# The second channel block of a causal depthwise convolution: from VectorE to GpSimd

## The reference, cut to what matters

```
def causal_dwconv(x, buf, w, b):
    xp = jnp.concatenate([buf.astype(x.dtype), x], axis=1)
    y = lax.conv_general_dilated(xp, w[:, None, :], window_strides=(1,), padding='VALID', ..., feature_group_count=x.shape[-1])
    return y + b.astype(x.dtype), xp[:, -(w.shape[0] - 1):]
...
glu = b_in[..., :W_B] * jax.nn.sigmoid(b_in[..., W_B:])          # W_B = 256
cb, nbuf_b = causal_dwconv(glu, buf_b, cm_dw_w[l], cm_dw_b[l])   # 31 taps
out_b = jax.nn.silu(layernorm_f32(cb.astype(jnp.float32), cm_ln_g[l], cm_ln_b[l]))
```

## Time and profile before

| what | value |
|---|---|
| median of 3 timed runs | 981.76 us (980.2 to 981.83) |
| span of the profiled execution | 979.8 us |
| outside that span, against the median | 2.0 us |
| TensorE busy | 922.9 us, 94% |
| VectorE busy | 453.6 us, 46% |
| GpSimd busy | 144.7 us, 15% |
| mean granted clock of TensorE | 0.974 |

### The profile page before, as it was taken

The page is one execution under the profiler, slowest core; times in us unless marked ns, Lnnn a source line. Parts: engine busy times, 40 slices in busy tenths (PEclk is TensorE's granted clock), DMA queues, the critical chain, the costliest instruction groups (busy, mean ns, idle before and its releaser), DMA issues.

```text
span 979.8 us, 13718 instructions
## 1 busy us (share of the span) xinstructions
PE 922.9 (94%) x5196; PEld 505.3 (52%) x5196; DVE 453.6 (46%) x1013; ACT 167.6 (17%) x357; POOL 144.7 (15%) x185
## 2 busy tenths in 40 slices
PE   7999779889999999999989997898799999999996
PEld 6744434675545545455476444347555554545552
DVE  3378794443343343434324887826224334343435
ACT  2213121201111111111211221211011111111113
POOL 0101110041112121211010001101311212121200
PEclk9999979899999999999999998899999999999999
DMA  9944622649999999993873055327499999999811
GB/s 301 312 167 188 165 87 60 237 153 372 378 390 359 389 374 373 398 360 142 280 235 129 1 218 128 92 43 306 173 389 391 386 389 374 379 388 358 341 65 49
DMA packets 100879, 252.76 MB, mean 258 GB/s; under 512 B 31682, under 2 KB 65494, under 8 KB 84438
## 3 DMA queue, kind: packets, MB, share of 16 engines
q1 hardware_dynamic: 73502, 239.45, 64.0%
q10 hardware_dynamic: 22728, 8.02, 3.6%
q0 software_dynamic: 4608, 4.73, 1.6%
HBM read 258.13 MB, written 6.52 MB: 270 GB/s over the span
## 4 chain that ended last, share of the span: by engine, by line
PE 76%; issue 13%; DVE 5%; ACTq 2%; DMA 1%; POOL 1%; ACT 1%; DVEq 0%; SPq 0%; POOLq 0%
PE psum L905 23%; PE psum L944 13%; PE psum L931 12%; PE psum L626 9%; PE psum L605 6%; PE psum L557 6%; PE psum L948 3%; ACTq L1745 2%; DVE cb L1168 2%; PE psum L637 1%; PE psum L563 1%; DMA rows<-xn_scratch,sg 1%; POOL v L1908 1%; DVE uT L1093 1%; PE psum L647 0%
## 5 line engine op out<-in xcount | busy, mean ns | idle before, releaser
L1537 DVE TENSOR_TENSOR x<-x,psum 128x512 f32<-128x512 f32 x128 | 88.1, 688 | 325.1 <-PE psum L944 325.1
L905 PE MATMUL psum<-ring,arena 128*64 128x256 f32 x1984 | 229.6, 385 | 2.8 <-DVE arena L1518 2.8
L905 PEld LDWEIGHTS psum<-ring,arena 128*64 128x64 f32 x1984 | 142.9, 138 | 88.0 <-issue 26.3
L944 PE MATMUL psum<-arena,kT 128*128 128x512 f32 x256 | 126.8, 618 | 0.0
L1930 POOL TENSOR_SCALAR kT<-const,sg 128x128 f32<-128x128 f32 (+1 forms) x96 | 65.2, 683 | 387.8 <-PE psum L948 387.6
L931 PE MATMUL psum<-ring,arena 128*64 128x512 f32 x496 | 116.8, 598 | 1.4 <-DVE arena L1528 1.4
L626 PE MATMUL psum<-ring,uT 128*128 128x512 f32 x256 | 112.8, 595 | 0.0
L626 PEld LDWEIGHTS psum<-ring,uT 128*128 128x128 f32 x256 | 47.8, 190 | 55.4 <-issue 54.5
L944 PEld LDWEIGHTS psum<-arena,kT 128*128 128x128 f32 x256 | 43.2, 189 | 57.0 <-issue 53.4
L1818 ACT ACTIVATE arena<-psum 128x256 f32<-128x256 f32 x64 | 24.5, 383 | 242.5 <-PE psum L905 242.5
L931 PEld LDWEIGHTS psum<-ring,arena 128*64 128x64 f32 x496 | 34.2, 136 | 61.0 <-issue 57.6
(11 more groups left out here) (268 smaller groups left out, 727.0 us busy)
## 6 DMA issues: line engine op xcount, KB each, us to landing
ring<-in_moe_w SPq DMA_DIRECT2D x186, 1024.0 KB, 8.0
ring<-in_w_in SPq DMA_DIRECT2D x24, 1024.0 KB, 11.7
ring<-in_w_out SPq DMA_DIRECT2D x8, 1024.0 KB, 6.4
arena<-in_state_ret ACTq DMA_DIRECT2D x16, 128.0 KB, 8.3
out<-arena ACTq DMA_DIRECT2D x16, 128.0 KB, 2.5
xn_scratch<-rows ACTq DMA_DIRECT2D x4, 512.0 KB, 5.7
uT<-in_moe_w SPq DMA_DIRECT2D x2, 1024.0 KB, 8.7
mixT<-in_moe_w SPq DMA_DIRECT2D x2, 1024.0 KB, 10.9
```

The costliest lines, as they stand in the source:

```text
L905: i = pe.matmul(b[64 * j:64 * j + 64, 0:FE], xsT[:, u // 2, k, s], w[j][:, k, :], start=k == 0, stop=k == KT - 1, skip_group_check=True)
L944: i = pe.matmul(b, back[:, pair, 128 * (a // 2):128 * (a // 2) + 128], ysb[:, 512 * (a % 2):512 * (a % 2) + 512], start=True, stop=True)
L1537: i = T(s, s, psum[:, b, :], ALU.add)
```

## The change

The taps of the second block over the prompt move from VectorE to GpSimd. VectorE keeps the first block, as one chain in which each tap waits for the one before it. GpSimd does each tap as two instructions: a product into one of two scratch pieces of 256 columns, and an addition to `cb`, with a wait for its own product between them. They stand behind the copies into `stg` and ahead of the scaling of the keys. The scratch lies in the second tile of `v`, so ScalarE waits for the last tap (`conv2_ready`) ahead of `values(1)`; TensorE waits for it ahead of the mean.

```diff
@@ -760,6 +761,7 @@
                 state(1)
                 pe.wait_ge(conv_ready, l + 1)
+                pe.wait_ge(conv2_ready, l + 1)
                 mean("lnm")
...
@@ -1153,19 +1155,15 @@
-                chain = [None, None]
-
                 def taps(k0, k1):
 
+                    dst = pr(cb[:, :])[:, 0, :]
                     for k in range(k0, k1):
-                        for c in range(2):
-                            w = P_(l, "dw", 2 * k + c)
-                            dst = pr(cb[:, :])[:, c, :]
-                            if k == 0:
-                                chain[c] = own(S(dst, glp[:, c, k:k + SEQ], w, P_(l, "db", c), ALU.mult, ALU.add))
-                            else:
-                                own.wait(chain[c])
-                                chain[c] = own(STT(dst, glp[:, c, k:k + SEQ], w, dst, ALU.mult, ALU.add))
+                        w = P_(l, "dw", 2 * k)
+                        if k == 0:
+                            do(S(dst, glp[:, 0, k:k + SEQ], w, P_(l, "db", 0), ALU.mult, ALU.add))
+                        else:
+                            do(STT(dst, glp[:, 0, k:k + SEQ], w, dst, ALU.mult, ALU.add))
...
@@ -1737,6 +1735,7 @@
+                act.wait_ge(conv2_ready, l + 1)
                 values(1)
...
@@ -1884,6 +1883,17 @@
+                dst = pr(cb[:, :])[:, 1, :]
+                for k in range(CONV_B):
+                    if k:
+                        product = vf[:, 512 + 256 * (k % 2):768 + 256 * (k % 2)]
+                        own(pool.tensor_scalar(product, glp[:, 1, k:k + SEQ], P_(l, "dw", 2 * k + 1), None, ALU.mult))
+                        own.wait()
+                        i = T(dst, dst, product, ALU.add)
+                    else:
+                        i = pool.tensor_scalar(dst, glp[:, 1, k:k + SEQ], P_(l, "dw", 2 * k + 1), P_(l, "db", 1), ALU.mult, ALU.add)
+                    i.then_inc(conv2_ready, 1) if k == CONV_B - 1 else own(i)
+
                 for t in (0, 2, 1):
                     n = TILES[t][1]
                     full(pool, l, f"tk{t}")
```

More of the change, by code:

```diff
@@ L362, in build @@
         bd_zero, count_read = sem("bd_zero"), sem("count_read")
+        conv2_ready = sem("conv2_ready")
         y_out, past_out = sem("y_out"), sem("past_out")
```

## The result

The changed kernel takes 1007.4 us against 981.8 us before in the same session: 1.0267 times as long, 95% interval 1.0241 to 1.0294. It is slower, as forecast, but by 25.6 us where 7.4 were forecast, and outside the range.

A forecast was written before the change was run, and what follows sets the result against it. TensorE, busy 94%, was taken as the bound, so only its waits count. Per layer 5.0 lateness + 1.0 clock - 2.3 shorter chain = +3.7; two layers +7.4 on 981.8 gave 989.2 us, range 976 to 1006.

The forecast's parts named there:

- the price of GpSimd's product: Each second-block tap on GpSimd: the 256-column multiplication takes 0.53 us, between bounds of 0.30 and 1.24.
- The disturbance: While the taps run on GpSimd, 41 VectorE instructions slow it by 0.17 us each, 8.5 us a layer with wide ones.
- The rival of a full exclusion: During the taps, VectorE and GpSimd instructions exclude each other entirely: 19.7 us, giving 1011 us; within a rival of chance 0.15.
- The lateness of `state(0)`: On TensorE, `state(0)` waits for the keys' scaling behind GpSimd's taps: 5.0 us late a layer, paid in full.
- The chain of seven taps: VectorE's last taps ahead of the mean take 6.4 us in place of 8.64, saving 2.3 us a layer.
- The clock: TensorE's granted clock may drop after the pause ahead of `state(0)`: 1.0 us a layer allowed.
- the third rival: GpSimd's taps are far slower, by a product at 0.9 us or full exclusion: 1011 us; chance 0.15.
- The addition: Second instruction of each GpSimd tap, 256 columns with two separate operands: 0.70 us.
- the rival that hung on a cheap addition: GpSimd's taps end in time, `state(0)` isn't late: 977.1 us, about 979 with additions at 0.56; chance 0.25.
- The cover of VectorE's waits: On VectorE, 21 us of idle and saved time a layer covers 16 us of waits on GpSimd.
- The waits of ScalarE and of the mean: The new waits on GpSimd's taps, ahead of copying `v1` and ahead of the mean, cost nothing by themselves.
- the rival says within 0.2%: Lateness of `state(0)` and VectorE's gain cancel within 2 us if GpSimd's taps end between 95.0 and 97; chance 0.13.

## Why the prediction was wrong

The sign, the place and the mechanism were right. The size was wrong, and one term of the sum carries it: the price of GpSimd's product.

**The product.** Taken at 0.53 us between bounds of 0.30 and 1.24; measured 0.92 to 0.93. That is 30 x 0.39 = 11.7 us a layer. It was priced from line 1870, which has two operations, plus an addend for the scalar. The run with two operations in the product showed 0.47, so that row was right for its own form; the product of the change has one operation, and that form was costlier, with a scalar per partition (0.92) as with a constant (0.85). Why one operation takes longer than two on GpSimd is not shown by any run. Both prices came from another form, since line 1930 has two operations as well, and I chose between them by what they compute. Yet the kernel before has a one-operation tensor_scalar with a scalar per partition, the comparison of line 1908 (groups by form: busy us, mean ns of one):

```profile
L1908 POOL TENSOR_SCALAR v<-const,sg 128x128 f32<-128x128 f32 x8 | 4.8, 617 | 117.6 <-DVEq L1476 117.6
```

It takes 0.62 us for 128 columns, more than the 0.53 that the prediction gave to 256. In proportion 256 columns would take 1.23, and less with a fixed part; 0.92 was measured. So this row of the right form spoke for the costly half of the range. It also shows that the number of operations is not the whole rule: at 128 columns the two operations of line 1930 took 0.79.

**The disturbance.** Forecast 8.5, measured 5.7 with the slow product and 8.1 with the fast one, so the estimate fits the kernel that it was made for. The rival of a full exclusion (19.7 us) is wrong: 5.7 is less than a third of it. Beside VectorE's eight taps from 65.76 to 71.14 (5.38 us, 0.67 each), GpSimd ran taps of 4.02/2 = 2.01 us in the changed kernel:

```profile
66.82 1.09 POOL L1890 TENSOR_SCALAR v<-glp,prm 128x256 f32<-128x256 f32 x1
...
70.84 1.09 POOL L1890 TENSOR_SCALAR v<-glp,prm 128x256 f32<-128x256 f32 x1
```

In these 4.02 us lie two of GpSimd's taps, 3.3 us of work when alone (0.92 + 0.72 each), and about six of VectorE's, 2.9 us when alone (0.48 each): 6.2 us of work in 4.0, so some 2 us of it ran at the same time. By the Trainium skill, "SBUF — State Buffer", section "Who interferes with whom", the two engines would exclude each other for whole instructions; the trace agrees only that they slow each other.

**The sum.** The lateness of `state(0)`: 5.0 forecast, 14.0 measured, since the taps take 57.7 and not 48.7 us (the product's 11.7 more, the disturbance 2.8 less). The chain of seven taps: 6.4 forecast, 6.25 measured, so 2.4 saved. The clock: 1.0 forecast; from `state(0)` to the matmuls behind the projection of `v1` TensorE takes 120.25 - 110.15 = 10.10 us, where it took 103.38 - 94.75 = 8.63, so 1.5 measured, and 1.9 in layer 1. The transfers gave 0.3 back in layer 0 (11.70 us of issuing in place of 12.07), which leaves 1.2 of it. The first profiled window behind the pause (length, busy us of the five engines, granted clock) shows the clock at its lower level of 1.2 GHz:

```profile
110.00:112.00 2.00, 1.85 (x20) 1.68 (x20) 0.43 (x1) 0.00 (x0) 1.04 (x2) 0.50 0.00 0
```

The forecast allowed 1.0 because a drop might come late or not at all behind a pause of 5.0 us. It came: the run with a pause of 5.93 us (tensor_tensor) and the one with 3.12 us (two operations) lost 2.5 and 1.7 us in the same stretch. Layer 0 is 14.0 + 1.2 - 2.4 = 12.8, twice that 25.6: this is the third rival, with its product of 0.9, to which I gave 0.15 and 1011 us, and whose worse half I left outside the range. In layer 1 `state(0)` waits as long:

```profile
607.54 1.12 PE L681 MATMUL psum<-v,kr 128*64 128x64 f32 x16 [14.25 <-issue]
```

**What held.** The addition at 0.72 (0.70 forecast; the estimate of 0.56 from the Trainium skill, "GPSIMD Engine Reference", section "Performance versus the Vector engine", is too low here, and the rival that hung on a cheap addition with it). The gap in front of an addition at 0.08. The cover of VectorE's waits: with GpSimd's 61 instructions in place and the keys early the kernel is 0.5% faster, and 0.7% without them, so that by the medians some 2 us of their cost in two layers reach the end, if any do. The waits themselves were forecast too high, 16 us a layer: VectorE is busy for 13.3 us more than without GpSimd's taps in both layers together (447.4 against 434.1), 6.7 a layer. The waits of ScalarE and of the mean at nothing, in the change as it stands.

Two of the rivals' conditions were worked out wrongly, without effect on the forecast. Half of the disturbance would end the taps at 98.7 - 4.25 = 94.5, not before 93.7. And taps that end at 97 would cost 3.3 + 1.0 - 2.3 = 2.0 us a layer, 0.4% for two, where the rival says within 0.2%.

**What was not seen.** That "a late `state(0)` is paid in full" held, since `v1` and the 1-MB transfers behind it move along. It does not hold for the copy of `v1` alone: with the keys early, 6 us of its lateness were given back by the transfers, a way to be wrong that the prediction had named. And the shorter chain was taken as the gain to be had, about 5 us, while taking the root ahead of the eight transfers was worth 13, on the same chain, where those transfers stand above the taps.

## What to carry to other kernels

Work given to an idle engine costs what stands behind it in that engine's order: put it behind, or let the urgent instruction through in its middle (here one moved instruction turned +2.7% into -0.4%). Price an instruction from a row of the same form, down to the number of operations and the kind of scalars, even where it computes something else (here the comparison of line 1908), and let the forecast's range reach well toward the upper bound where the rows disagree. Before shortening the last link of a waiting chain, look at what the chain waits for first: taking the root ahead of eight transfers was worth nearly three times what the split brought with the keys early.

## What the runs showed of the hardware

On GpSimd, with 128x256 elements, a tensor_scalar with one operation took 0.92 us (0.85 with a constant), with two operations 0.47, and the product as a tensor_tensor with a broadcast weight 0.60. With the constant a gap of 0.09 us stood ahead of each product, so that a tap was no shorter. Eight transfers of 128 KB kept ScalarE's queue, and ScalarE's next instruction, for 12 us (9.9 in layer 1) when SyncE issued two of 1 MB at the same moment, and for 5.5 us when they were issued 6.5 us behind those, and 6.9 us with the root ahead of them; whether the bytes on the way or the order of the issues makes the difference was not tried.
